# Feed-forward entry of the last block: the order of the low-part products and the engine that copies three weight pieces

## What is computed

```
x = x + rms_norm_2(mix, attn_post_norm[l])
h = rms_norm_2(x, ffn_pre_norm[l])
f = (jax.nn.silu(h @ w_gate[l]) * (h @ w_up[l])) @ w_down[l]
x = x + rms_norm_2(f, ffn_post_norm[l])
```

## Time and profile before

| | |
|---|---|
| median of 3 runs | 912.81 us (912.53 to 913.05) |
| profiled execution, its own time | 911.93 us |
| its span, first to last instruction | 909.8 us |
| mean granted TensorE clock | 0.997 of 2.4 GHz |
| TensorE matmul busy | 893.7 us (98%) |
| VectorE busy | 687.9 us (76%) |
| ScalarE busy | 284.6 us (31%) |
| GpSimd busy | 277.6 us (31%) |

### The profile page before, as it was taken

The page is one execution under the profiler, slowest core; times in us unless marked ns, Lnnn a source line. Parts: engine busy times, 40 slices in busy tenths (PEclk is TensorE's granted clock), DMA queues, the critical chain, the costliest instruction groups (busy, mean ns, idle before and its releaser), DMA issues.

```text
span 909.8 us, 12914 instructions
## 1 busy us (share of the span) xinstructions
PE 893.7 (98%) x4866; PEld 750.2 (82%) x4866; DVE 687.9 (76%) x726; ACT 284.6 (31%) x564; POOL 277.6 (31%) x180
## 2 busy tenths in 40 slices
PE   9999999999999999999999999999999899999997
PEld 7987798888887787798888888888867788888886
DVE  5889888777777876888777776767887687776774
ACT  3638271111113510463111112554685421111112
POOL 6410123444434431223444443100000254333331
PEclk9999999999999999999999999999999999999999
DMA  8960636555567455136555565376304266656541
GB/s 278 334 231 1 231 99 230 198 198 196 198 225 251 126 209 176 54 118 245 184 184 184 184 234 186 122 246 221 129 2 128 74 215 206 199 177 203 184 138 47
DMA packets 82407, 160.29 MB, mean 176 GB/s; under 512 B 5096, under 2 KB 40698, under 8 KB 82368
## 3 DMA queue, kind: packets, MB, share of 16 engines
q1 hardware_dynamic: 82208, 159.68, 51.5%
q10 hardware_dynamic: 160, 0.07, 0.0%
HBM read 158.68 MB, written 1.05 MB: 176 GB/s over the span
## 4 chain that ended last, share of the span: by engine, by line
PE 85%; DVE 6%; ACT 3%; DMA 3%; issue 2%; POOL 1%; DVEq 0%; POOLq 0%; SPq 0%; ACTq 0%
PE ps L2058 81%; PE ps L2062 3%; DMA raw<-in_odd_w_pw 2%; DVE w_lo L786 1%; DMA raw<-in_even_w_in 1%; ACT arena L1579 1%; DVE w_lo L984 1%; POOL w_hi L610 0%; POOL st L647 0%; ACT arena L1959 0%; DVE act_hl L994 0%; DVE x_res L879 0%; DVE arena L977 0%; ACT arena L1752 0%; POOL st L646 0%
## 5 line engine op out<-in xcount | busy, mean ns | idle before, releaser
L786 DVE TENSOR_TENSOR w_lo<-raw,w_hi 128x2048 fp32r<-128x2048 f32 (+2 forms) x138 | 315.7, 2311 | 39.6 <-POOL w_hi L767 21.8
L2058 PE MATMUL ps<-act_hl,w_hi 128*128 128x512 f32 (+1 forms) x1088 | 240.9, 367 | 1.3 <-DVE act_hl L994 0.6
L2058 PEld LDWEIGHTS ps<-act_hl,w_hi 128*128 128x128 f32 x1088 | 182.4, 189 | 31.3 <-issue 1.6
L2058 PE MATMUL ps<-w_hi,hl 128*128 128x512 f32 (+2 forms) x680 | 186.7, 384 | 0.6 <-DVE w_lo L786 0.6
L2058 PE MATMUL ps<-w_hi,act_hl 128*128 128x512 f32 (+3 forms) x656 | 180.8, 381 | 0.4 <-DVE act_hl L818 0.3
L625 POOL TENSOR_SCALAR w_hi<-raw 128x2048 fp32r<-128x2048 f32 x48 | 120.1, 2502 | 147.8 <-PE ps L2058 134.0
L2058 PEld LDWEIGHTS ps<-w_hi,hl 128*128 128x128 f32 (+1 forms) x680 | 125.7, 189 | 24.0 <-issue 0.8
L2058 PEld LDWEIGHTS ps<-w_hi,act_hl 128*128 128x128 f32 x656 | 118.6, 188 | 24.8 <-issue 3.1
L2058 PEld LDWEIGHTS ps<-act_hl,w_lo 128*128 128x128 f32 x960 | 129.1, 191 | 8.4 <-DVE w_lo L786 0.2
L2058 PE MATMUL ps<-act_hl,w_lo 128*128 128x256 f32 x960 | 132.4, 283 | 0.0
L2058 PE MATMUL ps<-w_lo,hl 128*128 128x512 f32 (+1 forms) x356 | 108.4, 378 | 0.0
(11 more groups left out here) (229 smaller groups left out, 765.9 us busy)
## 6 DMA issues: line engine op xcount, KB each, us to landing
raw<-in_mlp_w SPq DMA_DIRECT2D x64, 1024.0 KB, 5.3
raw<-in_w_gate SPq DMA_DIRECT2D x22, 512.0 KB, 3.9
raw<-in_w_up SPq DMA_DIRECT2D x22, 512.0 KB, 4.9
raw<-in_w_down SPq DMA_DIRECT2D x11, 1024.0 KB, 5.0
raw<-in_odd_w_pw SPq DMA_DIRECT2D x16, 512.0 KB, 5.9
raw<-in_w_in SPq DMA_DIRECT2D x8, 1024.0 KB, 6.5
raw<-in_even_w_in SPq DMA_DIRECT2D x4, 1024.0 KB, 10.4
raw<-in_even_w_out SPq DMA_DIRECT2D x4, 1024.0 KB, 7.3
```

The source lines that it names most:

```text
L786: tt(w_lo[slot_of(n)][:, 0:w], raw[slot_of(n)][:, 0:w], w_hi[slot_of(n)][:, 0:w].bitcast(F32), ALU.subtract).then_inc(S("w_split"), 1)
L2058: return pe.matmul(o, l, r, start=start, stop=stop, skip_group_check=True)
```

## The change

There are three edits, all at this entry.

TensorE (`wide_by_tile` with `lows_between=True`): the low-weight products are made tile by tile. Tile 0's 16 products with f0's low part stand ahead of tile 1's transposes, its 16 with f0+1's low part behind them; each is over 128 columns. The four unread products go. After tile 1's high-weight products, the last 32 low-weight ones are over 128 columns too (tile 1 alone).

VectorE (`boundary`, s = 5): the second half of f0+1's low part is made straight after the first half, ahead of `pre_tile(1)`, and no longer behind `low_tile(1)`. In the other boundaries nothing changes.

ScalarE and GpSimd: the high copies of f0+3, f0+4 and f0+5 go from GpSimd's loop (which now starts with its second turn, after a wait for those three) to ScalarE: f0+3 between `gate_half(0)` and `ff_hi(0)`, the other two behind `ff_hi(0)`.

```
 gpsimd:
                 boundary(5, f0 - 1)
-                with gp.Fori(0, FF_BLOCKS - 2) as i:
+                gp.wait_ge(S("w_hi"), f0 + 6)
+                with gp.Fori(1, FF_BLOCKS - 2) as i:
 vector, boundary():
                     lo_half(last + 2, 0)
+                    if s == 5:
+                        lo_half(last + 2, 1)
                     pre_tile(1, g + 1)
                     if s == 4:
                         lo_half(last + 2, 1)
                     low_tile(1, TURN_BANK[s])
-                    if s != 4:
+                    if s < 4:
                         lo_half(last + 2, 1)
 scalar:
                 gate_half(0, None)
+                hi(f0 + 3)
                 ff_hi(0)
+                hi(f0 + 4)
+                hi(f0 + 5)
 tensor, wide_by_tile():
+                        elif m == 1 and lows_between:
+                            arrived(n)
+                            low_part(n, slice(0, P), range(4))
+                            turn_m(turn_bank, 1)
+                            arrived(n + 1)
+                            low_part(n + 1, slice(0, P), range(4))
                         elif m == 1:
                             turn_m(turn_bank, 1)
                             keep_warm(turn_bank, 4)
...
                     arrived(n)
                     arrived(n + 1)
+                    toks = slice(P if lows_between else 0, T)
                     for c in range(4):
-                        low_part(n, slice(0, T), (c,))
-                        ins = low_part(n + 1, slice(0, T), (c,))
+                        low_part(n, toks, (c,))
+                        ins = low_part(n + 1, toks, (c,))
 tensor:
-                wide_by_tile(f0, ACC, out=True)
+                wide_by_tile(f0, ACC, out=True, lows_between=True)
```

More of the change, by code:

```diff
@@ L2176, in by_tile, with wide_by_tile @@
                     return v.rearrange("p (a t) -> p a t", a=2)[:, :, m * P:(m + 1) * P]
-                def wide_by_tile(n, turn_bank, out=False, halves_between=False):
+                def wide_by_tile(n, turn_bank, out=False, halves_between=False, lows_between=False):
                     def low_part(piece_, toks, cs):
```

## The result

The changed kernel takes 914.29 us (median of 22 runs, 910.88 to 916.72), the kernel before, run beside it, 911.94 us (22 runs, 910.21 to 913.75). The ratio is 1.0023, with a 95% interval of 1.0015 to 1.0032: slower by 2.1 us, or by 2.35 us if the two medians are subtracted. The forecast was 913.3 us with "no measurable change" as the likeliest case; the time lies in the stated range, 911.5 to 914.9, but it is a small loss and not a draw.

What follows compares the result with a forecast made beforehand. TensorE, busy without a break behind the entry, was taken as the bound, with two idle places in the entry. Terms +0.46, +0.85 and -0.85 gave 912.39 us profiled, 913.3 us as median; range 911.5 to 914.9 us.

Steps and rivals of the forecast that it cites:

- the sum: Whole entry: +0.46 + 0.85 - 0.85 = +0.46 us on the profiled 911.93 us, giving 912.39 us.
- sign of being wrong: In the changed trace: narrow products spaced off the 0.11 us floor, or a TensorE wait between 724 and 760 us.
- Edit 1: TensorE's low-weight products at the entry: narrow ones at 0.112 us each lengthen the path from 8.75 to 9.21 us, +0.46 us.
- (a): TensorE's narrow products lose the one-pass rate and cost 0.22 us each; 918.8 us, slower; chance 0.13.
- (b): TensorE's narrow products go by their columns, 0.060 us each; 910.8 us, just faster; chance 0.06.
- Edit 2: VectorE's half copy ahead of tile 1's norm holds GpSimd's L647, so `pre_tile` and the transposes come later, +0.85 us.
- Rival (c): Tile 1's norm chain: not held up, +0.30 us, 912.7 us, chance 0.18; or held twice, 913.6 us, chance 0.12.
- Edit 3: Three copies on ScalarE: TensorE's wait before the first down product goes, 0.76 us, and a short one, 0.08; -0.85 us.
- rival (d): Stall before the first down product stays, ScalarE late or VectorE gaining nothing; +1.3 us, 914.1 us; chance 0.10.
- the line on edit 1: TensorE around the transposes: 1.07 us go, 1.00 from 722.32 to 723.32 and a first gap 0.07 longer than 0.12.

Runs made afterwards that it cites:

- e1: Changed kernel plus six unread bfloat16 products in the idle time ahead of tile 1's transposes; 910.97 us, ratio 0.9998 to the kernel before.
- e11: Changed kernel run again unedited for one more trace; 910.50 us in its single run.
- e8: Changed kernel with the second half copy moved behind tile 1's norm, ahead of its low part; 911.50 us, ratio 1.0008 to the kernel before.
- e2: Kernel before with only the three high copies moved to ScalarE; 909.87 us, ratio 0.9991 to the kernel before.
- e7: Changed kernel with all 32 of tile 0's narrow products behind the transposes and 13 unread wide ones ahead; 912.46 us, ratio 1.0012 to the kernel before.
- e6: Kernel before without its four unread products behind the transposes; 912.18 us, ratio 1.0013 to the kernel before.
- e3: Kernel before with only the second half of f0+1's low part moved ahead of tile 1's norm; 913.27 us, ratio 1.0021 to the kernel before.
- e4: Changed kernel with the copies of f0+3 to f0+5 returned to GpSimd; 915.67 us, ratio 1.0052 to the kernel before.
- e9: Changed kernel with the four unread products put back behind the transposes; 912.97 us, ratio 1.0016 to the kernel before.
- e10: Kernel before with only the three high copies moved to ScalarE, run a second time; 910.21 us, ratio 0.9987 to the kernel before.

## Why the prediction was right and wrong

**The number: in the range, in part by luck.** The forecast of 913.3 us stands on the median of three runs, 912.81; 22 runs of the same kernel gave 911.94. From there the sum gives 912.4 us, 1.9 under the measured 914.29, and the range moved with it (910.6 to 914.0) would have missed. A base 0.9 us too high hid about half of a cost that the sum left out. The prediction's own sign of being wrong came up as well: in the first trace the second group of narrow products stood 0.215 us apart, off the floor, though for a reason that it did not name.

**Edit 1, +0.46 us: right.** The narrow products stand 0.111 us apart (0.112 taken). Rivals (a), 0.22, and (b), 0.060, are out: the 0.215 us of the second group in the first trace has the size of rival (a), but is the lower clock, as the same 16 products take 0.11 us in e1 and e11. The Trainium skill's 81 ns for such a stream ("TensorE: Matmul & The Clock Gate", section "Back-to-back issue gap") was not reached by these float32 weights.

**Edit 2, +0.85 us: right.** L647 took 1.43 us, ending 0.41 us after the half copy (720.33 and 719.92). From the first product of tile 0 to the transposes it is 721.17 - 714.08 = 7.09 us, against 721.16 - 714.86 = 6.30 in the earlier trace rows: +0.79. Rival (c) is out. e8 shows the cause from the other side.

**Edit 3, -0.85 us: right,** 0.84 in e2's distance; rival (d) is out. It is the one part worth having.

**The sum, +0.46 us: right for an execution at one clock.** The distance of e11 is 28.61 - 28.22 = +0.39 us, and the changed kernel's three executions at 0.999 took 910.9 to 911.0 us, against a median of 910.3 of the kernel before at 0.999 (12 executions beside e1 to e4).

**What failed** is the step from the sum to the time, and in it the line on edit 1 that books the four unread products and the wait by them, 1.07 us, as time that simply goes. I read "full granted clock" in the kernel before and did not ask what held it there. In 18 of 22 executions the changed kernel has a mean clock of 0.995 or less, median 914.5 us, and the one that was traced lost 3.16 us at 1.2 GHz. As an estimate, 18/22 of 3.16 us is 2.6 us on average. What is missing from the sum is 1.9 us by the medians and, taken from the means of the same runs (914.06 and 911.85), 1.75; the kernel before may lose something at this place as well, and only one of its executions was traced. So the clock has the right size for the whole of it, but the other 17 executions are put down to it by their mean clock and time alone.

Which part of the change lets the clock fall? Not the narrow products in themselves (e7). The loss of the unread products, with the 0.84 us of idle time that it bares, does so alone in part of the executions (e6, against 2 of 35 of the kernel before on the same chip), and so does the delayed norm (e3, against 1 of 29). Filling the idle time that was left keeps the clock up (e1, with e4 on the same chip as its opposite). The clock also fell less often with an undelayed norm (e8) and with the unread products restored (e9), but on other chips than the changed kernel's low runs can be shown for, so these two are only argued. The changed kernel had all of it at once: the norm delayed by 0.79 us, 1.36 us left idle behind the first narrow products, and the unread wide ones gone. What stays open is the exact condition: the clock of the same program, with the same waits, fell in one trace and not in two others, so something that these traces do not show decides each time. The clock even fell with the third edit alone (e10), where TensorE's work and waits up to that point are those of the kernel before.

## What to carry to other kernels

Before you remove work that "nobody reads" beside an idle stretch of TensorE, price the clock: look at the granted clock of the stretch behind it, and compare several executions, because one trace can show either case. Filling part of a gap with useful products over few columns neither makes them cheap (a pair of float32 weight load and product cost 0.11 us here, over 30 columns as over 128) nor need it hold the clock: with 1.36 us left idle behind them it fell, and it held when unread wide products filled that rest. And a VectorE operation with two SBUF inputs that is moved in front of a chain through GpSimd's tiny operations can hold up that chain until it is over (0.79 us here, for a copy of 1.2 us), even where its own queue has room.

## What I had not expected

- The clock fell while TensorE's longest idle time in the stage was 1.36 us (changed kernel), and held with 2.32 us in the traces of the kernel before and of e2. In e10, with 2.33 us, it fell. The Trainium skill ("TensorE: Matmul & The Clock Gate", section "HAM oscillation — how this bites in real kernels") speaks of idle gaps between bursts; here the length of the gap alone does not order the kernels.
- At the lower level narrow products saved nothing at all. The first ten of the 32 wide ones in the changed kernel's first trace stand (2.44 - 0.42) / 9 = 0.22 us apart, a longer first gap included (0.21 without it), and the narrow ones 0.215; at the upper level it is 0.12 and 0.111.

```profile
726.05 2.44 PE L2064 MATMUL ps<-act_hl,w_hi 128*128 128x256 f32 x10
```

- GpSimd's held operation gets in between two VectorE instructions that stand back to back (L646 took 0.45 us in e3 too), yet the next one, L647, then waits out the whole second instruction.
